# Dilated attention's transposes of p, product with V and read-out one chunk later, and modulation pieces spread anew over the steps

## The chip, the cores and the metric

The kernel runs on one core of a Trainium2 chip. The metric is the device time of one launch in microseconds (us). Five engines work from queues of their own, each strictly in its order, and wait for each other on semaphores: TensorE (PE in the profile, PEld its weight loads), VectorE (DVE), ScalarE (ACT), GpSimd (POOL) and SyncE (SP), which only issues transfers here.

## The reference, cut to what matters

Two transformer blocks over x of 256 rows and 2048 columns, in fp32. The change lies in the first, whose attention is this:

```python
mod = silu(c) @ w_ada + b_ada                       # six sections of 2048: the "modulation"
h = rms_norm(x, norm1_w) * (1 + scale1) + shift1
aq, ak, av, gq, gf, gi, gg = split(h @ w_in)        # 7 projections of 1024 columns
# 8 heads of 128; a query sees keys with a mask and a count (three dilated branches in one softmax)
p = exp(s - max(s)) * count ; o = (p @ V) / sum(p)
mix = concat(rms_norm(attn), hgrn2(gq, gf, gi, gg)) @ w_out
```

The remainder is a squared-ReLU MLP, a second block with another attention and another MLP.

## The kernel before

Weights come in chunks of 512 rows by 512 columns (1 MB). For each chunk ScalarE rounds it to w_hi (`split_hi`, L213), VectorE subtracts to get w_lo (`split_lo`, L217), and TensorE makes 24 matmuls with both (`chunk`, L227 to L229). There are four buffers, so in a step TensorE works on chunk x while the splits of chunk x+4, which take the buffer that x leaves, follow behind it.

The projection phase is a list of groups (`proj_groups`): two of HGRN2 with 16 chunks each (slots 0 to 15 and 16 to 31), then two of attention with 12 chunks each, at0 (slots 32 to 43) and at1 (slots 44 to 55). A slot is a step: one chunk on TensorE, one pair of splits. What was projected in a group is worked on in the steps of the next group: in at0's steps the second HGRN2 group runs its nine levels (`hg_stage`; level l stands on TensorE in step l, behind `grow` and copies on VectorE), in at1's steps the four heads of at0 run their softmax (`at_stage`), and the heads of at1 run it in `tail` (steps 2 to 11, slots 56 to 65), between the chunks of the output projection. After the tail VectorE squares MIX for a norm (L1133), and the late transposes and the rest of the output projection follow.

A head h of `at_stage` before the change: scores on TensorE in odd step 2h+1 (L1442, L1443); in even step 2h+2 the mask and maximum on VectorE (L1076 to L1081, signals s_max), exp on ScalarE (L626, L627), times count with the row sum on VectorE (L1085, signals p_rdy), and the three transposes of p on TensorE (L1458, wait for p_rdy); in step 2h+3 the copy of the transposes on ScalarE (L635) and the product with V (L1466 to L1468); in step 2h+4 the read-out on VectorE (L1058).

In every step an engine does its stage work first and its split after it, so ScalarE's w_hi stands behind exp, and VectorE's w_lo behind the softmax. In at0 and at1 the norm of Q or K (`head_norm`, L1008 to L1033) comes in steps 4 and 8, around that step's w_lo, with a power on GpSimd (L502) in it.

At the end of each step VectorE takes a number of modulation pieces (`ada_slot`: L902 for the first of 16, L905 for the others, 512 KB each from a ring of four that SyncE fills in order between the weight chunks). After every sixteenth piece come two collections (`ada_collect`, L890 and L892 twice). There are 96 pieces; `ada_pieces(slot)` says how many a slot has. SyncE loads x again only when all 96 are used.

Of the kernel before, what the change touches and what calls it, by code (L numbers as in the profile page):

```python
# [79 lines left out]
LEVEL_SLOTS = range(CH * 4, CH * 4 + 12), range(CH * 8, CH * 8 + 12)  # L80


def ada_pieces(slot):

    def before(x):
        return 3 * x // 2 if x <= CH * 4 else 3 * CH * 4 // 2 + 2 * (x - CH * 4) - sum(v < x for r in LEVEL_SLOTS for v in r)

    last = 2 * ADA_SLOTS
    return range(min(before(slot), last), min(before(slot + 1), last))
# [20 lines left out]
def build(nc, a, out):  # L110
    ctx = ExitStack()
    with ctx:
# [417 lines left out]
        def _(act):  # L530
# [75 lines left out]
            def at_stage(n, B0, s, stick):  # L606
                if s == 0:
                    act.wait_ge(chunk_done, 4 * (B0 + 3))
                    if isinstance(n, int) and n == 0:
# [4 lines left out]
                if s >= 2 and s % 2 == 0 and s <= 2 * GH:
# [13 lines left out]
                if s >= 3 and s % 2 == 1 and s <= 2 * GH + 1:  # L628
                    h = (s - 3) // 2
                    if stick:  # L630
                        act.wait_ge(arg_rdy, 4 * (n - AT_GROUPS) + h + 1)
                        act.activation(AMf[:, 0:384], AMf[:, 0:384], ACT.Exp).then_inc(pT_rdy, 1)
                    else:
                        act.wait_ge(pT_mm, 4 * n + h + 1)
                        act.activation(AMf[:, 0:384], bank(7, 0, 384), ACT.Copy).then_inc(pT_rdy, 1)  # L635
# [121 lines left out]
        def _(dve):  # L757
# [291 lines left out]
            def at_stage(n, s, stick, col):  # L1049
                d()  # L1050
                if s >= 4 and s % 2 == 0 and s <= 2 * GH + 2:
                    h = s // 2 - 2
                    dve.wait_ge(pv_mm, 4 * n + h + 1)
                    dst, src = MIX[:, :, col(h)], bank(7, 0, 2 * HD).rearrange("p (t d) -> p t d", t=T)
                    if stick:
                        dve.tensor_copy(dst, src).then_inc(pv_out, 1)
                    else:
                        dve.tensor_tensor(dst, src, rl[:, h % 2, :].unsqueeze(2).to_broadcast([P, T, HD]),  # L1058
                                          ALU.mult).then_inc(pv_out, 1)
                if s >= 2 and s % 2 == 0 and s <= 2 * GH:  # L1060
# [13 lines left out]
                    else:  # L1074
# [7 lines left out]
                        dve.wait_ge(p_exp, 4 * n + h + 1)  # L1082
                        for t, (c0, c1_) in enumerate(((0, 128), (128, 384))):
                            pp = E0f[:, 384 + c0:384 + c1_]
                            ins = dve.tensor_tensor_reduce(pp, pp, count[:, c0:c1_], 1.0, 0.0, ALU.mult, ALU.add,  # L1085
                                                           l_[:, t:t + 1])
                        ins.then_inc(p_rdy, 1)
                        d()
                        dve.reciprocal(rl[:, h % 2, :], l_[:, :])
                        d()  # L1090
# [247 lines left out]
        def _(pe):  # L1338
# [89 lines left out]
            def at_stage(n, s, stick):  # L1428
                if s >= 1 and s % 2 == 1 and s <= 2 * GH - 1:
# [6 lines left out]
                    if not (isinstance(n, int) and n == 0 and h == 0):  # L1436
                        pe.wait_ge(p_rdy, 4 * n + h)
# [231 lines left out]
```

## Time and profile before

| | |
|---|---|
| time, median of 3 runs | 2560.53 us (2560.37 to 2561.35) |
| the profiled execution | 2563.18 us, span 2561.1 us, mean TensorE clock 0.978 |
| TensorE busy | 2356.2 us (92%) |
| VectorE busy | 1673.7 us (65%) |
| ScalarE busy | 990.9 us (39%) |
| chain that ended last | TensorE 82%, VectorE 7% |
| mean w_lo (L217), w_hi (L213) | 2295 ns, 1915 ns |
| 1 MB of w_in from issue to landing (median) | 7.1 us |

Busy shares are of the span. A share is a mean over phases: TensorE sits still mostly in the first 700 us, in the phases that the change touches. An idle time behind a row is that of its engine just before it, with who ended it.

### The profile page before, as it was taken

The page shows a single profiled execution, that of the slowest core. Times are in us where ns is not written, and L with a number is a line of the kernel's source. Part 1 is how long each engine was busy: PE and PEld are TensorE (multiplying, and loading weights), DVE is VectorE, ACT ScalarE, POOL GpSimd, SP SyncE. Part 2 cuts the span into 40 slices and gives each one's busy share as a digit, 9 for nine tenths or more (in the row PEclk, how much of TensorE's full clock was granted, in tenths as well). Part 3 has the DMA queues.
Part 4 walks back from the last instruction along what each step waited for, and adds up shares of the span by engine and source line. Part 5 has one row for each costly group of instructions (what it writes and reads, how often), then busy time and mean ns, then how long its engine had stood idle before and what let it go on. Part 6 is the DMA issues. An engine that isn't in the chain of part 4 may idle for free.

```text
span 2561.1 us, 27768 instructions
## 1 busy us (share of the span) xinstructions
PE 2356.2 (92%) x10802; PEld 1955.8 (76%) x10802; DVE 1673.7 (65%) x1406; ACT 990.9 (39%) x745; POOL 60.1 (2%) x63
## 2 busy tenths in 40 slices
PE   0499989786899999999999999999999999999999
PEld 0488777665688888888887788877788888888887
DVE  7888797787656666665556755555765555555554
ACT  1143323233333333343433455565343334343332
POOL 0000000000000000000001200000000000000000
PEclk9999999888899999999999999999999999999999
DMA  7898575666466676755554454443555555555553
GB/s 315 329 356 298 186 262 203 204 211 214 133 215 232 228 244 232 243 190 187 191 186 148 164 179 161 158 158 115 161 198 186 193 185 194 184 193 184 193 185 110
DMA packets 230595, 519.14 MB, mean 203 GB/s; under 512 B 9402, under 2 KB 9859, under 8 KB 223875
## 3 DMA queue, kind: packets, MB, share of 16 engines
q1 hardware_dynamic: 230530, 518.27, 59.2%
q8 instruction: 42, 0.69, 0.1%
q14 instruction: 23, 0.18, 0.0%
HBM read 516.14 MB, written 2.10 MB: 202 GB/s over the span
## 4 chain that ended last, share of the span: by engine, by line
PE 82%; DVE 7%; issue 3%; ACT 2%; DMA 2%; DVEq 2%; POOL 1%; POOLq 0%; ACTq 0%; SPq 0%
PE PS L227 26%; PE PS L229 26%; PE PS L228 26%; DMA ada_raw<-in_w_ada_dram 2%; PE PS L1372 2%; ACT w_hi L213 1%; DVE ada_acc L905 1%; DVE MS L865 1%; PE PS L1405 1%; DVE GN L303 1%; POOL rstd L502 0%; DVEq L971 0%; PE PS L264 0%; DVE A_lo L311 0%; DVE w_lo L217 0%
## 5 line engine op out<-in xcount | busy, mean ns | idle before, releaser
L217 DVE TENSOR_TENSOR w_lo<-raw,w_hi 128x2048 fp32r<-128x2048 f32 x392 | 898.6, 2295 | 758.9 <-ACT w_hi L213 757.0
L213 ACT ACTIVATE w_hi<-raw 128x2048 fp32r<-128x2048 f32 x392 | 749.9, 1915 | 1172.4 <-PE PS L229 1160.8
L227 PE MATMUL PS<-w_hi,A_hi 128*128 128x512 f32 x2112 | 839.7, 398 | 21.9 <-DVE A_lo L311 15.7
L229 PE MATMUL PS<-w_hi,A_lo 128*128 128x512 f32 x2112 | 828.7, 392 | 0.0
L228 PE MATMUL PS<-w_lo,A_hi 128*128 128x512 f32 x2112 | 828.5, 392 | 0.0
L227 PEld LDWEIGHTS PS<-w_hi,A_hi 128*128 128x128 f32 x2112 | 401.7, 190 | 106.2 <-DVE A_lo L311 15.9
L229 PEld LDWEIGHTS PS<-w_hi,A_lo 128*128 128x128 f32 x2112 | 400.3, 190 | 84.9
L228 PEld LDWEIGHTS PS<-w_lo,A_hi 128*128 128x128 f32 x2112 | 401.4, 190 | 81.5 <-issue 0.5
L227 PE MATMUL PS<-w_hi,H_hi 128*128 128x512 f32 x1024 | 402.8, 393 | 0.1
L229 PE MATMUL PS<-w_hi,H_lo 128*128 128x512 f32 x1024 | 399.2, 390 | 0.0
L228 PE MATMUL PS<-w_lo,H_hi 128*128 128x512 f32 x1024 | 398.8, 389 | 0.0
L229 PEld LDWEIGHTS PS<-w_hi,H_lo 128*128 128x128 f32 x1024 | 192.5, 188 | 40.4
L227 PEld LDWEIGHTS PS<-w_hi,H_hi 128*128 128x128 f32 x1024 | 192.6, 188 | 39.8 <-issue 0.9
L228 PEld LDWEIGHTS PS<-w_lo,H_hi 128*128 128x128 f32 x1024 | 192.7, 188 | 39.5 <-issue 0.5
L905 DVE SCALAR_TENSOR_TENSOR ada_acc<-X,sc,ada_acc 128x1024 f32<-128x1024 f32 x90 | 115.3, 1281 | 3.8 <-DVE ada_acc L905 0.3
L1355 PE MATMUL PS<-ones,MS 128*128 128x1 f32 x64 | 13.9, 352 | 89.9 <-DVE MS L865 89.9
L1355 PEld LDWEIGHTS PS<-ones,MS 128*128 128x128 f32 x64 | 13.8, 332 | 90.2 <-issue 58.0
L865 DVE SCALAR_TENSOR_TENSOR MS<-ada_raw,sc,MS 128x2048 f32<-128x2048 f32 x30 | 70.5, 2351 | 3.8 <-DMA ada_raw<-in_w_ada_dram 1.6
L1218 DVE TENSOR_TENSOR X<-X,PS 128x1024 f32<-128x1024 f32 x60 | 72.8, 1214 | 0.0
L1218 DVE TENSOR_TENSOR ACC<-ACC,PS 128x1024 f32<-128x1024 f32 x60 | 72.8, 1214 | 0.0
L288 ACT ACTIVATE A_hi<-GN 128x512 fp32r<-128x512 f32 x24 | 15.1, 629 | 117.7 <-DVE GN L303 117.7
L502 POOL TENSOR_TENSOR rstd<-ssq,mhalf 128x8 f32<-128x8 f32 x19 | 33.1, 1742 | 1075.5 <-DVE ssq L328 1075.5
(250 smaller groups left out, 1175.3 us busy)
## 6 DMA issues: line engine op xcount, KB each, us to landing
raw<-in_w_ff_dram SPq DMA_DIRECT2D x128, 1024.0 KB, 5.2
raw<-in_mlp_w_in_dram SPq DMA_DIRECT2D x64, 1024.0 KB, 5.4
raw<-in_mlp_w_out_dram SPq DMA_DIRECT2D x64, 1024.0 KB, 4.9
raw<-in_w_in_dram SPq DMA_DIRECT2D x56, 1024.0 KB, 7.1
X<-in_w_ada_dram SPq DMA_DIRECT2D x96, 512.0 KB, 5.3
raw<-in_sb_w_qkv_dram SPq DMA_DIRECT2D x48, 1024.0 KB, 5.0
ada_raw<-in_w_ada_dram SPq DMA_DIRECT2D x32, 1024.0 KB, 7.2
raw<-in_w_out_dram SPq DMA_DIRECT2D x16, 1024.0 KB, 8.4
```

Source lines behind the costliest of these rows:

```text
L213: act.activation(w_hi[:, j, :, :], raw[:, j, :, :], ACT.Copy).then_inc(hi_rdy, 1)
L217: dve.tensor_tensor(w_lo[:, j, :, :], raw[:, j, :, :], w_hi[:, j, :, :].bitcast(F32), ALU.subtract).then_inc(lo_rdy, 1)
L227: pe.matmul(bank(pair + t), h, w_hi[:, j, k, :], start=first, stop=False)
L228: pe.matmul(bank(pair + t), h, w_lo[:, j, k, :], start=False, stop=False)
L229: mm = pe.matmul(bank(pair + t), l, w_hi[:, j, k, :], start=False, stop=last)
L303: ins = dve.tensor_scalar(tmp[:, pos % 2, S * k:S * k + S], bank(banks[pos % len(banks)], S * k, S * k + S), g[:, kt:kt + 1], s[:, kt:kt + ...
L502: pool.tensor_tensor(rstd[:, :], ssq[:, :], mhalf[:, :], ALU.pow).then_inc(rstd_rdy, 1)
L865: ins = dve.scalar_tensor_tensor(out=MS[:, h, :], in0=sl, scalar=sc[:, k:k + 1], in1=MS[:, h, :], op0=ALU.mult, op1=ALU.add)
L905: ins = dve.scalar_tensor_tensor(out=acc, in0=ada_ring[:, q % CH, :], scalar=sc[:, k:k + 1], in1=acc, op0=ALU.mult, op1=ALU.add)
L1218: dve.tensor_tensor(ac, ac, PS[:, b:b + 2, :], ALU.add).then_inc(acc_read, 1)
L1355: mm = pe.matmul(bank(6, KT * h + k, KT * h + k + 1), MS[:, h, k * P:k * P + P], ones[:, 0:1], start=True, stop=True)
L1372: mm = pe.transpose(bank(first_bank + i, P * q, P * q + P), src[:, t, HD * h:HD * (h + 1)], ident[:, :])
```

## The change

Part one: for the dilated attention (stick is False) `lag = s - 1` takes the place of s for count and row sum (VectorE), the transposes of p, the product with V (TensorE), the copy between them (ScalarE, now ahead of exp in a step) and the read-out (VectorE). Scores, mask, maximum and exp keep their steps, and the scores now wait for s_max in place of p_rdy. Part two: a table gives the pieces of each slot.

```diff
-LEVEL_SLOTS = range(CH * 4, CH * 4 + 12), range(CH * 8, CH * 8 + 12)
+PIECES = (1, 2) * 8 + \
+         (2, 1, 1, 1, 1, 1, 1, 1, 1, 1, 1, 0, 2, 3, 2, 3) + \
+         (2, 1, 1, 1, 0, 1, 1, 1, 0, 1, 2, 2) + \
+         (2, 2, 1, 2, 0, 2, 1, 2, 0, 2, 2, 2) + \
+         (2,) * 9 + (1,)
...
+    return range(sum(PIECES[:slot]), sum(PIECES[:slot + 1]))
...
@@ ScalarE, at_stage (the same block stood behind exp before)
+                lag = s if stick else s - 1
+                if lag >= 3 and lag % 2 == 1 and lag <= 2 * GH + 1:
+                    h = (lag - 3) // 2
...
+                        act.wait_ge(pT_mm, 4 * n + h + 1)
+                        act.activation(AMf[:, 0:384], bank(7, 0, 384), ACT.Copy).then_inc(pT_rdy, 1)
@@ VectorE, at_stage
-                if s >= 4 and s % 2 == 0 and s <= 2 * GH + 2:
-                    h = s // 2 - 2
+                lag = s if stick else s - 1
+                if lag >= 4 and lag % 2 == 0 and lag <= 2 * GH + 2:
+                    h = lag // 2 - 2
...
-                        dve.wait_ge(p_exp, 4 * n + h + 1)
-                        for t, (c0, c1_) in enumerate(((0, 128), (128, 384))):
...
+                if not stick and lag >= 2 and lag % 2 == 0 and lag <= 2 * GH:
+                    h = lag // 2 - 1
+                    dve.wait_ge(p_exp, 4 * n + h + 1)
+                    for t, (c0, c1_) in enumerate(((0, 128), (128, 384))):
@@ TensorE, at_stage
-                        pe.wait_ge(p_rdy, 4 * n + h)
+                        pe.wait_ge(p_rdy if stick else s_max, 4 * n + h)
...
-                if s >= 2 and s % 2 == 0 and s <= 2 * GH:
-                    h = s // 2 - 1
+                lag = s if stick else s - 1
+                if lag >= 2 and lag % 2 == 0 and lag <= 2 * GH:
+                    h = lag // 2 - 1
...
-                if s >= 3 and s % 2 == 1 and s <= 2 * GH + 1:
-                    h = (s - 3) // 2
+                if lag >= 3 and lag % 2 == 1 and lag <= 2 * GH + 1:
+                    h = (lag - 3) // 2
```

Before, slots 0 to 15 had 1 and 2 in turn as now, slots 16 to 27 and 32 to 43 had 1, slots 28 to 31 and 44 to 63 had 2. So the pieces of the second HGRN2 group go from 20 to 22, those of at0 from 12 to 13, of at1 from 24 to 18, of the tail from 16 to 19. The collections behind pieces 31, 47, 63, 79 and 95 move: from slot 23 to 22, from 35 to 32 (at0, step 3 to step 0), from 47 to 46 (at1, step 3 to step 2), from 55 to 57 (at1's last step to the tail), from 63 to 65.

VectorE at the turn from the last HGRN2 projection steps to at0, before: the first row is the splits of slot 31, the last the first level copy of step 1.

```order
L217 TENSOR_TENSOR w_lo<-raw,w_hi 128x2048
L905 SCALAR_TENSOR_TENSOR ada_acc<-X,sc,ada_acc 128x1024 x2
L217 TENSOR_TENSOR w_lo<-raw,w_hi 128x2048
L905 SCALAR_TENSOR_TENSOR ada_acc<-X,sc,ada_acc 128x1024
L970 TENSOR_TENSOR GN<-PS,GN 128x1024
L983 TENSOR_TENSOR AM<-PS,ident 128x1024
```

And VectorE at the same place in the changed kernel (line numbers are one higher there).

```order
L217 TENSOR_TENSOR w_lo<-raw,w_hi 128x2048
L906 SCALAR_TENSOR_TENSOR ada_acc<-X,sc,ada_acc 128x1024 x3
L217 TENSOR_TENSOR w_lo<-raw,w_hi 128x2048
L906 SCALAR_TENSOR_TENSOR ada_acc<-X,sc,ada_acc 128x1024 x2
L891 STREAM_TRANSPOSE rt<-ada_acc 128x512
L893 TENSOR_REDUCE ada_part<-rt 128x16
L891 STREAM_TRANSPOSE rt<-ada_acc 128x512
L893 TENSOR_REDUCE ada_part<-rt 128x16
L971 TENSOR_TENSOR GN<-PS,GN 128x1024
L984 TENSOR_TENSOR AM<-PS,ident 128x1024
```

Two more pieces and a pair of collections stand ahead of step 1's copy; one more piece is added in slot 29.

VectorE in at1 from step 2 on (first head of at0), before.

```order
L1076 TENSOR_TENSOR E<-PS,maskadd 128x384
L1078 TENSOR_REDUCE mx<-E 128x1
L1079 TENSOR_REDUCE mx<-E 128x1
L1081 TENSOR_SCALAR nmx<-mx 128x2
L1085 ISA E,l_<-E,count 128x128
L1085 ISA l_ 128x1
L1085 ISA E,l_<-E,count 128x256
L1085 ISA l_ 128x1
L1089 RECIPROCAL rl<-l_ 128x2
L217 TENSOR_TENSOR w_lo<-raw,w_hi 128x2048
L905 SCALAR_TENSOR_TENSOR ada_acc<-X,sc,ada_acc 128x1024 x2
```

VectorE at the same place in the changed kernel.

```order
L1083 TENSOR_SCALAR nmx<-mx 128x2
L217 TENSOR_TENSOR w_lo<-raw,w_hi 128x2048
L906 SCALAR_TENSOR_TENSOR ada_acc<-X,sc,ada_acc 128x1024
L891 STREAM_TRANSPOSE rt<-ada_acc 128x512
L893 TENSOR_REDUCE ada_part<-rt 128x16
L891 STREAM_TRANSPOSE rt<-ada_acc 128x512
L893 TENSOR_REDUCE ada_part<-rt 128x16
L1089 ISA E,l_<-E,count 128x128
L1089 ISA l_ 128x1
L1089 ISA E,l_<-E,count 128x256
L1089 ISA l_ 128x1
L1093 RECIPROCAL rl<-l_ 128x2
```

The product with count (now L1089), which the transposes wait for, has moved behind a w_lo, one piece and a pair of collections.

## Rows read from the trace of the kernel before

**Rows 1.** Timeline of TensorE, first matmul after a stall: start, us, shape, [idle <- releaser].

```profile
280.80 1.41 PE L1401 MATMUL PS<-bT,kT 128*128 128x128 f32 x5 [3.37 <-DVE AM L989]
...
346.04 2.05 PE L1405 MATMUL PS<-bT,kT 128*128 128x128 f32 x16
...
363.71 2.05 PE L1405 MATMUL PS<-bT,kT 128*128 128x128 f32 x16 [2.92 <-DVE kT L963]
...
376.94 3.78 PE L1405 MATMUL PS<-bT,kT 128*128 128x128 f32 x16 [5.71 <-DVE kT L963]
...
445.48 0.90 PE L1458 MATMUL PS<-ident,E 128*128 128x128 f32 x3 [3.95 <-DVE l_ L1085]
...
467.85 0.90 PE L1458 MATMUL PS<-ident,E 128*128 128x128 f32 x3 [6.80 <-DVE l_ L1085]
...
487.04 0.90 PE L1458 MATMUL PS<-ident,E 128*128 128x128 f32 x3 [4.46 <-DVE l_ L1085]
...
505.97 0.88 PE L1458 MATMUL PS<-ident,E 128*128 128x128 f32 x3 [3.61 <-DVE l_ L1085]
```

**Rows 2.** Timeline of TensorE inside two chunks.

```profile
413.49 0.39 PE L228 MATMUL PS<-w_lo,A_hi 128*128 128x512 f32 x1
413.72 0.39 PE L229 MATMUL PS<-w_hi,A_lo 128*128 128x512 f32 x1
...
447.03 0.63 PE L229 MATMUL PS<-w_hi,A_lo 128*128 128x512 f32 x1
447.46 0.63 PE L227 MATMUL PS<-w_hi,A_hi 128*128 128x512 f32 x1
```

**Rows 3.** Seven stretches, TensorE: length, busy, granted clock, DMA share, GB/s.

```profile
280.80:284.00 3.20, 3.20 (x12) 0.50 0.02 5
376.90:383.00 6.10, 6.06 (x22) 0.50 0.41 116
...
sum 30.60, PE 30.51; mean PE 4.36
```

**Rows 4.** Groups of instructions on VectorE from 424 to 600 us.

```profile
L905 DVE SCALAR_TENSOR_TENSOR ada_acc<-X,sc,ada_acc 128x1024 f32<-128x1024 f32 x39 | 50.0, 1282 | 2.5 <-DVE ada_acc L905 0.3
```

**Rows 5.** Timeline of VectorE, around a pair of collections.

```profile
461.28 0.71 DVE L890 STREAM_TRANSPOSE rt<-ada_acc 128x512 f32<-128x512 f32 x1
...
464.47 0.42 DVE L1058 TENSOR_TENSOR MIX<-PS,rl 128x256 f32<-128x256 f32 x1
```

**Rows 6.** Timeline of VectorE in at0, steps 2 and 4.

```profile
344.69 0.69 DVE L962 TENSOR_TENSOR bT<-bT,E 128x512 f32<-128x512 f32 x1
...
366.54 2.28 DVE L217 TENSOR_TENSOR w_lo<-raw,w_hi 128x2048 fp32r<-128x2048 f32 x1
```

**Rows 7.** One stretch: length, busy of PE, PEld, DVE, ACT, POOL, clock, DMA, GB/s.

```profile
326.00:346.00 20.00, 20.00 (x105) 16.86 (x103) 19.33 (x15) 6.66 (x4) 0.00 (x0) 1.00 0.96 362
```

**Rows 8.** Timeline of GpSimd: the powers in steps 4 and 8 of at0.

```profile
366.71 3.61 POOL L502 TENSOR_TENSOR rstd<-ssq,mhalf 128x8 f32<-128x8 f32 x1 [63.49 <-DVE ssq L328]
...
403.92 1.64 POOL L502 TENSOR_TENSOR rstd<-ssq,mhalf 128x8 f32<-128x8 f32 x1 [33.59 <-DVE ssq L328]
```

**Rows 9.** Timeline of VectorE in at1, steps 2 and 4.

```profile
442.42 0.56 DVE L1076 TENSOR_TENSOR E<-PS,maskadd 128x384 f32<-128x384 f32 x1
...
444.78 0.29 DVE L1085 CUSTOM_DVE_ANT_0 E<-E,count 128x128 f32<-128x128 f32 x1 [0.87 <-ACT E L627]
...
446.58 2.29 DVE L217 TENSOR_TENSOR w_lo<-raw,w_hi 128x2048 fp32r<-128x2048 f32 x1 [0.90 <-ACT w_hi L213]
...
472.07 1.22 DVE L1014 TENSOR_TENSOR QN<-PS,rstd 128x1024 f32<-128x1024 f32 x1
...
476.45 0.75 DVE L902 TENSOR_SCALAR ada_acc<-X,sc 128x1024 f32<-128x1024 f32 x1
```

**Rows 10.** Timeline of VectorE: start of the tail, and its end.

```profile
539.26 0.99 DVE L303 TENSOR_SCALAR GN<-PS,gmix,zero_c 128x256 f32<-128x256 f32 x2
...
598.43 1.23 DVE L1133 CUSTOM_DVE_ANT_0 QN<-MIX 128x1024 f32<-128x1024 f32 x1 [0.22 <-issue]
```

More of the change, by code:

```diff
@@ L77 @@
 WO_ORDER = [(b, k) for b in range(3) for k in (0, 1, 2)] + [(b, 3) for b in range(3)] + [(3, k) for k in range(4)]
-LEVEL_SLOTS = range(CH * 4, CH * 4 + 12), range(CH * 8, CH * 8 + 12)
+PIECES = (1, 2) * 8 + \
[3 rows of a table added]
+         (2,) * 9 + (1,)
 def ada_pieces(slot):
[L85 to L89, printed above, removed]
+    return range(sum(PIECES[:slot]), sum(PIECES[:slot + 1]))
 def ada_collected(slot):
@@ L613, in at_stage @@
                     from_pair(VN, 2, ACT.Copy, stick).then_inc(pair_read[2], 1)
+                lag = s if stick else s - 1
+                if lag >= 3 and lag % 2 == 1 and lag <= 2 * GH + 1:
+                    h = (lag - 3) // 2
+                    if stick:
+                        act.wait_ge(arg_rdy, 4 * (n - AT_GROUPS) + h + 1)
+                        act.activation(AMf[:, 0:384], AMf[:, 0:384], ACT.Exp).then_inc(pT_rdy, 1)
+                    else:
+                        act.wait_ge(pT_mm, 4 * n + h + 1)
+                        act.activation(AMf[:, 0:384], bank(7, 0, 384), ACT.Copy).then_inc(pT_rdy, 1)
                 if s >= 2 and s % 2 == 0 and s <= 2 * GH:
@@ L627, in at_stage @@
                         act.activation(E0f[:, 512:768], E0f[:, 128:384], ACT.Exp, bias=nmx[:, 1:2]).then_inc(p_exp, 1)
-                if s >= 3 and s % 2 == 1 and s <= 2 * GH + 1:
-                    h = (s - 3) // 2
[L630 to L635, printed above, removed]
             act.wait_ge(rstd_rdy, POWER_OF[0])
@@ L1081, in at_stage @@
                         dve.tensor_scalar(nmx[:, :], mx[:, :], -1.0, None, ALU.mult).then_inc(s_max, 1)
-                        dve.wait_ge(p_exp, 4 * n + h + 1)
-                        for t, (c0, c1_) in enumerate(((0, 128), (128, 384))):
[L1084 to L1090, printed above, removed]
+                if not stick and lag >= 2 and lag % 2 == 0 and lag <= 2 * GH:
+                    h = lag // 2 - 1
+                    dve.wait_ge(p_exp, 4 * n + h + 1)
+                    for t, (c0, c1_) in enumerate(((0, 128), (128, 384))):
+                        pp = E0f[:, 384 + c0:384 + c1_]
+                        ins = dve.tensor_tensor_reduce(pp, pp, count[:, c0:c1_], 1.0, 0.0, ALU.mult, ALU.add,
+                                                       l_[:, t:t + 1])
+                    ins.then_inc(p_rdy, 1)
+                    d()
+                    dve.reciprocal(rl[:, h % 2, :], l_[:, :])
+                    d()
                 if stick and s >= 3 and s % 2 == 1 and s <= 2 * GH + 1:
@@ L1459, in at_stage @@
                     mm.then_inc(pT_mm, 1)
-                if s >= 3 and s % 2 == 1 and s <= 2 * GH + 1:
-                    h = (s - 3) // 2
+                if lag >= 3 and lag % 2 == 1 and lag <= 2 * GH + 1:
+                    h = (lag - 3) // 2
                     cols = slice(HD * h, HD * (h + 1))
```

## The prediction

> **What bounds the kernel now.** I read the shares first: TensorE is busy 92% of the span and 82% of the chain that ended last, so almost all of the launch is matmul time that the change doesn't touch. What can move is TensorE's idle time. So next comes the timeline of TensorE with the idle time before each row, in the phases that the change edits. Each stall there ends with VectorE: one in the second HGRN2 group (3.4 us), two in at0 (levels 4 and 5: 2.9 and 5.7 us), four in at1 at the transposes of p (4.0, 6.8, 4.5, 3.6: 18.9 us) [rows 1]. Level 2 in at0, at 346.04, has no idle time before it [rows 1], though VectorE ran its `grow` for it only from 344.69 [rows 6]: VectorE arrives just in time there, with nothing to spare.
>
> A stall costs twice. Between two matmuls of a chunk there are 0.23 us at the full clock and 0.43 us in the step after the stall at 445.48 [rows 2]; seven stretches behind such stalls, 30.6 us in all, ran at half the granted clock (1.2 of 2.4 GHz), 4.4 us each on the mean [rows 3]. By the two intervals a stretch loses 0.47 of its length, so 2.05 us on the mean. The stall of 2.92 us was followed by no such stretch, that of 3.37 us was [rows 1, 3]. The four stalls in at1 with 18.0 us of low clock behind them thus cost 18.9 + 8.5 = 27.4 us. The Trainium skill (TensorE: Matmul & The Clock Gate, Part 1) puts the penalty at the throttled time times one half; by that a stretch would lose 2.2 us and the four in at1 9.0 us, which alters no sign below.
>
> VectorE's prices: a piece is 1.28 us busy [rows 4], 1.4 with its gap; a pair of collections takes 3.2 us [rows 5]; a w_lo 2.2 us from start to next start (table above: 2.295 busy); mask and maximum 1.5 us (442.42 to 444.78 less the 0.87 idle), count and row sums 0.7 us until TensorE's transposes at 445.48 [rows 1, 9]; norm, gain and rotation of Q or K after the w_lo 4.4 us [rows 9]. On ScalarE exp takes 0.85 us (VectorE's idle 0.87 [rows 9]) and w_hi 1.9 us (table). A chunk is 24 matmuls at 0.227, 5.45 us. Scores, transposes and product with V take about 0.5, 0.45 and 0.7 us; each is there as often after as before, so their price doesn't enter, only where they stand.
>
> **The second HGRN2 group.** The pair of collections moves from slot 23 to 22. The stall of 3.4 us before level 8 goes and one of the same 3.2 us comes before level 7, which waits for a copy that follows these collections. Sum 0. Its one more piece in slot 16 meets steps with VectorE waiting for w_hi, so it costs nothing; if that cover were gone, 1.4 us.
>
> **at0, a loss.** Three pieces (slots 29, 31, 32; one each) and a pair of collections (from step 3 to step 0) now stand before VectorE's step 1. VectorE is busy 19.3 of 20 us from 326 to 346 [rows 7], so all of it delays: 3 x 1.4 + 3.2 = 7.4 us; the piece of step 1 is then the first of its sixteen, 0.5 us shorter. `grow` of level 2 ends 6.6 to 6.9 us later, and TensorE, which was ready at 346.04, waits: +6.6, and +2.05 for the clock. Behind it level 4 no longer waits (-2.9), since the collections that made it wait are gone from step 3. Level 5 waits for all of step 4: from the end of chunk 3 VectorE needs w_hi 2.0, w_lo 2.2, piece 1.4, level work 1.4 and 1.4, squares 1.5, w_lo 2.2, a pause of 1.5, norm 4.4 and `grow` 1.2 = 19.2; TensorE needs twice a chunk and a level, 14.5. So 4.7 to 5.0 us of stall in place of 5.7, with the same low clock (-0.7). Sum: 6.6 + 2.05 - 2.9 - 0.7 = +5.05.
>
> The pause of 1.5 us is one place to weigh a rule. The power on GpSimd that began with a w_lo just under way took 3.61 us, another that began ahead of its w_lo took 1.64 [rows 6, 8]. The Trainium skill (SBUF — State Buffer, Who interferes with whom) says that VectorE and GpSimd share one pair of ports under an exclusive lock; the first row agrees with that. By the rule the pause stays, as w_hi of that step is ready before VectorE comes; by the row of 1.64 it would go, and the sum for at0 would be +3.5.
>
> **at1, a gain.** I carry the queues forward on the old clock of the trace. The one piece more of slots 42 and 43 uses up two pauses before w_lo and leaves VectorE 0.8 us late at the mask: 443.2. s_max 444.7, exp 445.55, w_hi 447.45 (VectorE has only this to wait for: 2.75 us idle in place of 0.87 + 0.90), w_lo 449.65, one piece and the collections 454.25, count and sums: p_rdy at 454.95. TensorE ends chunk 2 at 441.5 (445.48 less 3.95), chunk 3 and the scores at 447.45. It waits 7.5 us, where it waited 4.0 a step earlier: the chunk of cover is eaten by w_lo, piece and collections. Then at half clock for a while: chunk 4 ends 462.9, and chunk 5 with product and scores 469.5; VectorE: w_hi 464.9, w_lo 467.1, norm 471.5, read-out and sums 472.5, a wait of 3.0. In the same way: steps 6 and 7 without a norm, p_rdy 486.6 against 485.05, a wait of 1.55; steps 8 and 9 with the norm of K, 504.7 against 498.65, a wait of 6.05. Together 18.1 us, hardly less than 18.9, but only two of the four are long enough for the low clock for sure (4.1 us in place of 8.5); the one of 3.0 lies between 2.9 and 3.4, and I count half a stretch, 1.0 us. Sum up to step 9: 18.1 + 4.1 + 1.0 - 27.4 = -4.2. The pair of collections that stood in the last step, right before the tail's first transform, moves into the tail: -3.2. Sum -7.4.
>
> **The tail, a loss.** From its first VectorE row to the squares of MIX are 59.2 us [rows 10], nearly all VectorE's queue. It gets three pieces (4.15 us) and a pair of collections (3.2) more; all stand before the squares. The four waits for exp (3.5 us) and four for w_hi go (3.8 us); after the mask in steps 4 and 6 and in step 3 there are waits for w_hi of 2.7, 2.7 and 1.4. Sum: 7.35 - 7.3 + 6.8 = +6.85. TensorE has no chunk left to do from step 8 on, so nothing covers this. After the tail nothing is changed. SyncE's reload of x and the weights behind it wait for piece 96; it now comes about 0.6 us later relative to the squares, while the first split behind the reload stands after a norm and four transforms: nothing.
>
> **Sum.** 0 + 5.05 - 7.4 + 6.85 = +4.5 us. The profiled execution (2563.18 us, 2.65 above the median) would take 2567.7; the median 2565.0. A measurement of this kernel tells about 0.2%, 5.1 us, from no change; +4.5 is just inside.
>
> **Bounds.** A low-clock stretch is between 3.2 and 6.1 us long, so each of the six in question may cost 1.5 to 2.9: about +-1.5 in all. If the 3.0 us wait keeps the full clock, -1.0. Small restart costs of each stall that I left out: -1. At the turn to at0 three-piece slots make SyncE, which serves the ring and the weights in one order, issue weight loads later: 1 MB takes 7.1 us to land (table), and the DMA engines are 0.96 busy from 326 to 346 us already [rows 7]. If the loads for slots 34 to 36 land late, VectorE's full queue gets up to 3 us longer.
>
> **Rivals.** (1) At0 costs little: if VectorE had slack before level 2 that I don't see, at most 5.05 goes and the sum is -0.5: 2560.0. Against it: no idle time between `grow` at 344.69 and the level at 346.04 [rows 1, 6]. (2) The other side, faster: the extra chunk covers the K norm in step 9. If VectorE comes to its product there 6 us earlier than I count, the wait of 6.05 and its low clock (2.05) go, the sum is -3.6; it decides for faster from the point on where the waits of steps 3 or 5 also go, together -8 to -14: 2550. For it: the wait is a difference of two long queues, and one chunk more is what the transposes get. Against: before, the wait with the norm of Q in the same step was the longest [rows 1], and w_hi behind exp keeps VectorE idle longer than before. (3) Slower: the loads of slots 34 to 36 come late as above and each new stall draws the longest low clock: +3, +3.5: +11, 2571.5. (4) The lag does nothing because all depends on the pieces: then at1 gives only -3.2, and the sum is +8.7, 2569.
>
> **Chances.** The forecast (+2 to +7) 0.5, half a step under the 5.1 us border, so 0.27 within and 0.23 slower; (1) 0.16 within; (2) 0.13, faster; (3) and (4) 0.21, slower. That is 0.13 faster, 0.43 within, 0.44 slower. The range leaves out the far part of (2) and (3): 2556 to 2571.
>
> **What would show it.** TensorE: a new stall of 6 to 7 us before level 2 in at0 (near 353 us), none before level 4; in at1 waits for L1089's signal in steps 3, 5, 7, 9 of about 7.5, 3, 1.5 and 6 us; the tail's first transform on VectorE about 2 us earlier than 539.3, and the squares 66 us after it, near 603. VectorE idle about 2.7 us before w_lo in steps 2 and 6 of at1. Wrong would be: no stall at level 2, a wait in step 9 under 3 us, or a tail under 63 us.

## The result, and the profile after

The changed kernel took 2572.09 us (median of 6 runs, 2570.87 to 2574.16), the kernel before 2561.38 beside it: ratio 1.004, 95% interval 1.003 to 1.005. It is 10.7 us slower; the forecast was +4.5. The profiled execution took 2572.91 us, its span 2570.9 us. The instructions are as many as before. TensorE is busy 2.1 us longer and stands still 7.7 us longer (the span less its busy time, 212.6 us after 204.9):

```profile
span 2570.9 us, 27768 instructions
...
PE 2358.3 (92%) x10802; PEld 1958.8 (76%) x10802; DVE 1674.2 (65%) x1406; ACT 991.6 (39%) x745; POOL 62.0 (2%) x63
```

The timeline of TensorE in the kernel after, the first matmul behind each wait (the counterpart of [rows 1]; columns as there):

```profile
273.08 3.44 PE L1409 MATMUL PS<-bT,kT 128*128 128x128 f32 x16 [3.66 <-DVE AM L990]
...
354.19 3.78 PE L1409 MATMUL PS<-bT,kT 128*128 128x128 f32 x16 [8.60 <-DVE kT L964]
...
383.43 3.78 PE L1409 MATMUL PS<-bT,kT 128*128 128x128 f32 x16 [5.03 <-DVE kT L964]
...
461.50 0.90 PE L1463 MATMUL PS<-ident,E 128*128 128x128 f32 x3 [7.47 <-DVE l_ L1089]
...
479.10 0.90 PE L1463 MATMUL PS<-ident,E 128*128 128x128 f32 x3 [3.34 <-DVE l_ L1089]
...
494.56 0.56 PE L1463 MATMUL PS<-ident,E 128*128 128x128 f32 x3
...
513.96 0.90 PE L1463 MATMUL PS<-ident,E 128*128 128x128 f32 x3 [7.19 <-DVE l_ L1089]
```

Two things are to be seen. Level 2 of at0, which waited for nothing before, waits 8.60 us; level 4 has no wait any more, level 5 has 5.03. In at1 the four waits at the transposes are now three, 18.0 us together against 18.8 [rows 1], though each transpose has a chunk of matmuls more ahead of it.

VectorE's timeline gives the start and the end of the tail (counterpart of [rows 10]): 67.21 us where there were 59.17. The row between them is the tail's first w_lo.

```profile
539.49 0.99 DVE L303 TENSOR_SCALAR GN<-PS,gmix,zero_c 128x256 f32<-128x256 f32 x2
...
554.40 2.29 DVE L217 TENSOR_TENSOR w_lo<-raw,w_hi 128x2048 fp32r<-128x2048 f32 x1 [2.94 <-ACT w_hi L213]
...
606.70 1.23 DVE L1137 CUSTOM_DVE_ANT_0 QN<-MIX 128x1024 f32<-128x1024 f32 x1 [0.22 <-issue]
```

Part by part, from the same events in both traces (a part is how much later its last event comes, less what the parts before it added):

| part | forecast | measured | from which events |
|---|---|---|---|
| second HGRN2 group | 0 | -0.45 | w_hi at 289.08, after 288.63 |
| at0 | +5.05 | +6.9 | at1's first scores 435.25, after 441.66 |
| at1 | -7.4 | -6.2 | tail's first transform 539.26, after 539.49 |
| tail | +6.85 | +8.0 | 59.17 and 67.21 us |
| behind the tail | 0 | +1.6 | first transpose of ACC 678.54, after 688.37 |
| sum | +4.5 | +9.8 | |

The three parts with a forecast other than 0 have its sign: the two that cost came out dearer, and the one that pays paid less. Behind the tail, where nothing was forecast, 1.6 us came. The forecast 2565.0 missed by 7.1 us, 1.1 beyond its range. Of these, 0.85 us are the kernel before, whose median beside this one is 2561.38 and not 2560.53; as a difference the forecast is 6.2 us off. The two traces differ by 9.8 us and the medians by 10.7, because the profiled execution of the kernel before took 1.8 us more than its median and that of the kernel after 0.8.

Two readings show the excess. First, ScalarE's timeline ahead of the new wait in at0, and VectorE's beside it:

```profile
327.53 1.92 ACT L213 ACTIVATE w_hi<-raw 128x2048 fp32r<-128x2048 f32 x1 [5.11 <-DMA raw<-in_w_in_dram]
337.10 1.92 ACT L213 ACTIVATE w_hi<-raw 128x2048 fp32r<-128x2048 f32 x1 [6.74 <-DMA raw<-in_w_in_dram]
...
339.05 2.29 DVE L217 TENSOR_TENSOR w_lo<-raw,w_hi 128x2048 fp32r<-128x2048 f32 x1 [1.73 <-ACT w_hi L213]
```

w_hi waits for a transfer of weights (five do between 320 and 348 us; in the kernel before none does from 260 to 700 us), and VectorE, in a stretch in which it was to be full, waits 1.73 us for w_hi. Second, TensorE's granted clock. Stretches of the kernel before (columns as in [rows 7]) at the tail's first chunk and behind the tail:

```profile
543.50:550.50 7.00, 6.99 (x24) 5.66 (x25) 5.39 (x15) 1.46 (x4) 0.00 (x0) 0.75 0.00 0
604.50:614.50 10.00, 8.43 (x36) 6.79 (x37) 7.45 (x13) 6.51 (x8) 0.00 (x0) 0.80 0.76 295
```

and the same two places in the kernel after:

```profile
543.70:550.70 7.00, 6.95 (x18) 5.47 (x19) 6.27 (x11) 1.49 (x4) 0.00 (x0) 0.56 0.21 65
612.70:622.70 10.00, 8.45 (x29) 6.69 (x30) 7.40 (x13) 6.52 (x8) 0.00 (x0) 0.56 0.83 321
```

In 7 and 10 us it did 24 and 36 matmuls before, 18 and 29 after: at mean clocks of 0.56 instead of 0.75 and 0.80. The waits ahead of these places were 8.95 and 12.71 us before, 7.48 and 13.87 after, nearly the same. What differs is how long the half clock lasts behind them.

### The profile page after: what moved, and what is told of

Its sections match the earlier page's. It is cut to its first block, busy times and chain, and to the rows that moved or that the text cites. A ratio compares the mean times of both kernels' runs of the same rounds, so it can differ in the third digit from the quotient of the medians.

```text
span 2570.9 us, 27768 instructions
## 1 busy us (share of the span) xinstructions
PE 2358.3 (92%) x10802; PEld 1958.8 (76%) x10802; DVE 1674.2 (65%) x1406; ACT 991.6 (39%) x745; POOL 62.0 (2%) x63
## 4 chain that ended last, share of the span: by engine, by line
PE 80%; DVE 8%; issue 4%; ACT 2%; DMA 2%; DVEq 2%; POOL 1%; POOLq 0%; ACTq 0%; SPq 0%
PE PS L227 25%; PE PS L229 25%; PE PS L228 25%; DVE ada_acc L906 2%; ACT w_hi L213 2%; PE PS L1376 2%; DVE MS L866 1%; DMA ada_raw<-in_w_ada_dram 1%; PE PS L1409 1%; DVE GN L303 1%; DVE w_lo L217 1%; POOL rstd L502 0%; DVEq L890 0%; PE PS L264 0%; DVE A_lo L311 0%
```

## The experiments

Each was timed beside the kernel before, whose median stood between 2561.1 and 2561.7 us; the kernel after is 2572.1. Each kernel has one trace; where a run's times scatter widely, its trace need not stand for its median.

### One half of the change at a time

e1 has the lag alone, with the pieces of before:

```diff
-PIECES = (1, 2) * 8 + \
...
+LEVEL_SLOTS = range(CH * 4, CH * 4 + 12), range(CH * 8, CH * 8 + 12)
...
```

> The kernel before with the lag of one chunk alone: transposes, product with V and read-out come a chunk later, the modulation pieces stay where they were. Theory (the lag pays only together with its spread, since the queue of VectorE between two masks doesn't get shorter): carrying the queues forward with the old spread gives waits of TensorE at the transposes in at1 of 4.9, 8.4, 1.4 and 8.9 us, 23.6 in all against 18.9 before, one low-clock stretch fewer, and a tail about 1 us longer; at0 and the second HGRN2 group as before. Sum about +3.5 on the kernel before: 2565. Rival (the chunk of cover is worth something by itself): the four waits shrink by more than 5 us in all with their low-clock stretches, 2556 or less. The kernel after stood at 2572.1.

It took 2565.56 us (ratio 1.0017, 1.0008 to 1.0026). The timeline of TensorE in e1, in at1:

```profile
452.53 0.90 PE L1463 MATMUL PS<-ident,E 128*128 128x128 f32 x3 [4.68 <-DVE l_ L1089]
...
475.91 0.90 PE L1463 MATMUL PS<-ident,E 128*128 128x128 f32 x3 [7.78 <-DVE l_ L1089]
...
491.38 0.55 PE L1463 MATMUL PS<-ident,E 128*128 128x128 f32 x3 [1.24 <-DVE l_ L1089]
...
512.44 0.90 PE L1463 MATMUL PS<-ident,E 128*128 128x128 f32 x3 [8.89 <-DVE l_ L1089]
```

22.6 us against 18.8, where 23.6 was forecast: the theory's queues hold within a microsecond. The lag alone costs 4.0 us.

e2 has the table of pieces alone, in the order of before:

```diff
-LEVEL_SLOTS = range(CH * 4, CH * 4 + 12), range(CH * 8, CH * 8 + 12)
+PIECES = (1, 2) * 8 + \
+         (2, 1, 1, 1, 1, 1, 1, 1, 1, 1, 1, 0, 2, 3, 2, 3) + \
...
```

> The kernel before with the new table of modulation pieces alone; transposes, product and read-out stay where they were. Theory (the spread makes the loss, in at0 and the tail, and the lag gives little back): at0 +6.5 to +8.5 at level 2 as in the kernel after, the tail about 3 pieces and a pair of collections longer (+6 to +7), at1's waits of TensorE shorter only by the collections taken out (-3): 2569 to 2571. Rival (the lag makes the loss): 2563 or less.

2569.53 us (1.0021 to 1.0048): the spread alone costs 8.0 us. Its wait at level 2 was 8.70 us (8.60 after), and its tail 66.1 us (67.2 after). The halves together would be +12.0, and both are +10.7: each loses by itself, and they give each other back little.

### What stands ahead of level 2

```diff
-         (2, 1, 1, 1, 1, 1, 1, 1, 1, 1, 1, 0, 2, 3, 2, 3) + \
+         (2, 1, 1, 1, 1, 1, 1, 1, 1, 2, 1, 1, 2, 2, 2, 2) + \
```

> The kernel after with no slot of three pieces: two pieces of the last steps before at0's first chunks go to earlier steps of the second HGRN2 group. The slots from 16 on are 2 1 1 1 1 1 1 1 1 2 1 1 2 2 2 2 instead of 2 1 1 1 1 1 1 1 1 1 1 0 2 3 2 3. Theory (two pieces of VectorE's full queue and the late weight loads behind the threes make a part of at0's new stall at level 2): VectorE no longer idles 1.7 us for w_hi before level 2, and its queue has two pieces (2.8 us) less there; the stall of 8.6 us becomes 4 to 5, and the time falls by 4.5 to 2567.6. Rival (it comes back as a stall in the second HGRN2 group or at level 5, where TensorE waits for VectorE anyway): 2571 to 2572.

2566.86 us: 5.2 less than after, 4.5 forecast. The wait at level 2 fell from 8.60 to 4.19 us, and nothing came back in the HGRN2 group (3.65 us in place of 3.66).

e4 leaves the table and moves the piece loads behind the next weight load on SyncE:

```diff
                     load(B, j, w_in[:, j, :, c0:c0 + NC_])
-                    if B:
-                        for q in ada_pieces(CH * (B - 1) + j):
+                    if B and CH * (B - 1) + j:
+                        for q in ada_pieces(CH * (B - 1) + j - 1):
                             ada_load(q)
...
```

> The kernel after with one thing changed on SyncE: the loads of a slot's modulation pieces are issued one weight load later, so that the weight load of the next step stands ahead of them in the ring. Theory (weight loads late behind nine piece loads of three slots hold ScalarE's w_hi at 337.10 by 6.74 us and leave VectorE idle 1.73 us before level 2): ScalarE's w_hi there no longer waits for a transfer, the stall before level 2 is 6.9 instead of 8.6 us, time 2570.4. Rival (the transfers are bound by the DMA engines, and order alone moves no weight earlier; or the loads of the pieces are then late themselves): no change, 2572, or a new wait of VectorE for a piece.

No w_hi waited for a transfer any more, and the wait at level 2 was 6.96 us, 0.06 from the forecast of 6.9:

```profile
353.74 3.77 PE L1412 MATMUL PS<-bT,kT 128*128 128x128 f32 x16 [6.96 <-DVE kT L967]
```

So the late weights make 1.64 us of that wait. The median, 2571.34 us, is only 0.75 below after, too little to be told from nothing. e17 below makes the same edit where more is late.

### The clock

e5 keeps TensorE busy in its wait behind the tail; `warm(k)` is k transposes of the identity into bank 6:

```diff
...
+            pe.wait_ge(s_max, 4 * AT_GROUPS)
+            warm(20)
             pe.wait_ge(pv_out, 4 * AT_GROUPS)
+            warm(65)
+            pe.wait_ge(rstd_rdy, POWER_OF[1])
+            warm(10)
             turn(1, MIX, steps=LATE1, first=len(EARLY1), banks=NARROW)
```

> The kernel after, and TensorE does idle work (95 transposes of the identity matrix into bank 6, which nobody reads) in the 13.9 us in which it waits for the squares of MIX at the end of the tail, in three groups held back by signals that it waits for anyway. Nothing else waits for them. Theory (1.6 us behind the tail are low clock: in the kernel after the first 3.7 us of the chunk behind this wait ran at half clock, in the kernel before none of it): the chunk runs at the full clock from its start, from the first transpose of MIX to those of ACC 74.0 us in place of 75.6, time 1.6 to 2.2 below the kernel after: 2570.2. Rival (the chunk is held by VectorE's splits and the queue behind it, not by TensorE's clock): less than 0.5 us, 2571.7 or more.

2573.7 us, nothing gained. The idle work did lift the clock inside the wait, but it fell again right at the chunk. Stretches of e5:

```profile
602.00:612.00 10.00, 8.20 (x74) 7.76 (x73) 7.07 (x12) 0.31 (x1) 1.64 (x1) 1.00 0.70 267
...
612.90:617.90 5.00, 2.50 (x18) 1.70 (x16) 4.01 (x8) 3.10 (x6) 0.00 (x0) 1.00 1.05 408
618.60:622.00 3.40, 3.40 (x9) 2.63 (x8) 2.19 (x5) 2.89 (x3) 0.00 (x0) 0.50 0.71 275
```

Between the idle work and the chunk TensorE has only the 16 transposes of MIX, with pauses: busy 2.5 of 5 us. Behind these the clock was low for 3.4 us, in the chunk, where the kernel after has 3.5 us of low clock. So the run tells nothing about the price of the low clock there; it shows that this idle work, which ended 5 us ahead of the chunk, did not shorten the low clock in it.

e6 does the same inside at1's waits, where the next work follows at once:

```diff
...
             def at_stage(n, s, stick):
+                if isinstance(n, int) and n == 0 and not stick and s in (3, 5, 9):
+                    pe.wait_ge(s_max, 4 * n + s // 2)
+                    warm({3: 60, 5: 24, 9: 60}[s])
```

> The kernel after, and TensorE does idle work (transposes of the identity into bank 6, 60, 24 and 60 of them) ahead of the scores in steps 3, 5 and 9 of at1, within its waits of 7.5, 3.3 and 7.2 us, so that its clock doesn't fall behind them. In the kernel after 14.2 us behind these three waits ran at half clock, by the two intervals of [rows 2] 6.7 us. Theory (the time lost to the clock is in part time that TensorE would wait for VectorE in the next step: the queue of VectorE sets the steps, and only what is lost behind the last wait, or what VectorE waits for in turn, is paid): waits become longer by part of it, 3.5 to 4.5 us are gained, 2568. Rival (as the prediction reckoned, a low-clock stretch adds in full to its wait): 6.7 us, 2565.4. Other rival (VectorE alone sets at1): under 1 us, 2571.5.

2568.84 us (8 runs, 2564.51 to 2573.01). Stretches of the kernel after behind its three waits:

```profile
461.50:464.60 3.10, 3.10 (x9) 2.62 (x10) 2.99 (x3) 0.49 (x1) 0.00 (x0) 0.50 0.73 274
479.10:485.00 5.90, 5.90 (x16) 4.75 (x17) 5.52 (x6) 0.49 (x1) 0.00 (x0) 0.50 0.16 28
514.00:519.20 5.20, 5.20 (x18) 4.62 (x19) 4.93 (x4) 1.58 (x3) 0.00 (x0) 0.50 0.07 9
```

and the same places in e6:

```profile
462.30:465.40 3.10, 3.09 (x15) 2.61 (x16) 2.98 (x3) 0.49 (x1) 0.00 (x0) 1.00 0.79 297
480.00:485.90 5.90, 5.90 (x21) 4.75 (x22) 5.55 (x6) 0.49 (x1) 0.00 (x0) 0.71 0.19 33
513.60:518.80 5.20, 5.20 (x29) 4.50 (x30) 4.93 (x4) 1.58 (x3) 0.00 (x0) 1.00 0.10 17
```

65 matmuls in place of 43 in the same 14.2 us. A half clock of 3.4 us stayed behind the second wait (the mean of 0.71), so 10.8 us of low clock went, worth 5.1 us at 0.47. Gained were 3.3 us by the medians and 4.3 by the trace, from the transposes in step 3 to the squares (145.2 to 140.9 us). The first theory's 3.5 to 4.5 fits better than the full price, but the runs of e6 scatter over 8.5 us, and the trace is of the slowest of them: the 76.9 us from the first transpose of MIX to those of ACC are the most of all traces here, and its whole span, 2571.0 us, is that of the kernel after. So this is a hint and not a proof that a part of each low-clock stretch is time that TensorE would have waited anyway.

### Who eats the chunk of cover

The change moved the count and the read-out on VectorE along with TensorE's transposes: the count now stands behind w_lo, the pieces and the collections of its step. e9 undoes that part alone:

```diff
             def at_stage(n, s, stick, col):
-                lag = s if stick else s - 1
-                if lag >= 4 and lag % 2 == 0 and lag <= 2 * GH + 2:
-                    h = lag // 2 - 2
+                if s >= 4 and s % 2 == 0 and s <= 2 * GH + 2:
+                    h = s // 2 - 2
...
-                if not stick and lag >= 2 and lag % 2 == 0 and lag <= 2 * GH:
-                    h = lag // 2 - 1
+                if not stick and s >= 2 and s % 2 == 0 and s <= 2 * GH:
+                    h = s // 2 - 1
```

> The kernel after with one part of the lag undone: on VectorE count, row sums and read-out stay in the steps of before (right behind the mask, ahead of w_lo and pieces); on TensorE and ScalarE transposes, the copy of p and the product come a chunk later, the pieces are spread as after. Theory (the chunk of cover is eaten because the same edit puts VectorE's count behind w_lo, the pieces and a read-out that itself comes late): TensorE's waits in at1 shrink from 18 us to 6 or 7 (half of that moves to the scores, which wait for the mask), and the time falls to 2560 to 2562. Rival (VectorE's queue is full in at1, so that its order is all the same): waits of 15 us or more, 2569 or more. Other rival (VectorE now waits for the product in the step in which it reads it out, up to 10 us in the tail): 2572 or more.

2559.4 us: 12.7 less than after, and level with before (ratio 0.9994, 0.9985 to 1.0003). TensorE's timeline in at1 of e9, the four transposes and, of the scores, the two that wait:

```profile
453.06 0.49 PE L1462 MATMUL PS<-ident,E 128*128 128x128 f32 x3
...
466.24 0.49 PE L1445 MATMUL PS<-kT,qT 128*128 128x128 f32 x2 [1.07 <-DVE nmx L1082]
...
467.76 0.55 PE L1462 MATMUL PS<-ident,E 128*128 128x128 f32 x3 [0.59 <-DVE l_ L1088]
...
483.38 0.49 PE L1445 MATMUL PS<-kT,qT 128*128 128x128 f32 x2 [3.45 <-DVE nmx L1082]
...
484.89 0.90 PE L1462 MATMUL PS<-ident,E 128*128 128x128 f32 x3 [0.50 <-DVE l_ L1088]
...
498.11 0.49 PE L1462 MATMUL PS<-ident,E 128*128 128x128 f32 x3
```

5.6 us of waits in place of 18.0, where 6 to 7 were forecast. From the first scores of at1 to the tail's first transform e9 takes 82.6 us, the kernel after 97.8. In the tail VectorE waits once 3.23 us for the product, and the tail is 1.4 us longer than after. A chunk of cover is worth a chunk once the signal that it covers isn't put off by the same edit. e10 is the same with the pieces of before:

```diff
-PIECES = (1, 2) * 8 + \
...
+LEVEL_SLOTS = range(CH * 4, CH * 4 + 12), range(CH * 8, CH * 8 + 12)
```

> The kernel before with transposes, copy of p and product a chunk later on TensorE and ScalarE alone; VectorE's order and the pieces as before. Theory as for e9: the four waits of TensorE at the transposes in at1 (18.9 us before) come down to under 2 us, 3 to 6 us come back as waits for the mask, and waits behind the last K norm grow (one of 5 to 8 us before the tail's first chunk): 5 to 6 us below the kernel before, 2555.5, and 10 below the lag with VectorE in it (e1, 2565.6). Rival (any lag costs): 2562 or more.

2558.28 us, 7.3 less than e1, 2.9 under before, where 5 to 6 were forecast. Its waits at the transposes in at1 are 2.1 us in all, but its tail takes 63.9 us, with a wait for the count of 9.54 us.

e13 and e15 take the lag out of the tail, in the kernel after and in e10 (the first pair of lines wherever it stands):

```diff
-                lag = s if stick else s - 1
+                lag = s if stick or n else s - 1
-                        pe.wait_ge(p_rdy if stick else s_max, 4 * n + h)
+                        pe.wait_ge(p_rdy if stick or n else s_max, 4 * n + h)
```

> The kernel after with the lag in at1 only: in the tail (the second attention group, after the last projection step) transposes, copy, product, count and read-out stand in the steps of before. Theory (with no chunk of projection behind it, the lag in the tail costs VectorE about 1 us, and it is also what makes the chunk behind the tail run its first 3.7 us at half clock): tail 1 us shorter, from the first transpose of MIX to those of ACC 74.0 us in place of 75.6, time 2569.4 (2.7 less than after). Rival (the clock behind the tail falls as it does by chance of its place in time): 2571.

2571.21 us, tail 67.0 us: in the kernel after the lag costs the tail next to nothing, and the rival was right. The half clock behind the tail stayed though this lag was gone, so it doesn't need it.

> The order of e10 in at1, the order of before in the tail, the pieces as before. e10 had a wait of 9.5 us for count in its tail (the kernel before 4.9) and 75.7 us from the first transpose of MIX to those of ACC (before 74.0). Theory (both come of the lag in the tail, where no chunk covers anything): 4 us less tail and 1.6 us less behind it, 2552.7 (5.6 under e10's 2558.3, 8.5 under before). Rival (the tail's lag costs nothing, VectorE's queue there is full anyway): 2557 to 2558.

2552.71 us (ratio 0.997, 0.9959 to 0.9981), where 2552.7 was forecast; its seven times lie between 2550.2 and 2557.2, so that the match to the hundredth is luck. In e10 the tail's count stands early on VectorE while TensorE takes it up late; there the lag did cost (tail 59.1 us in place of 63.9).

### What the spread is worth

e7 is the kernel before with another table, e8 the kernel after with one, e12 a second table for the order of before, e11 one for the order of e10, e14 one for that of e15. Each table was found for its own order, by carrying the queues forward. The edit in all is of this kind (here e11, in the kernel of e9; the other tables stand in the expectations):

```diff
-         (2, 1, 1, 1, 1, 1, 1, 1, 1, 1, 1, 0, 2, 3, 2, 3) + \
-         (2, 1, 1, 1, 0, 1, 1, 1, 0, 1, 2, 2) + \
-         (2, 2, 1, 2, 0, 2, 1, 2, 0, 2, 2, 2) + \
-         (2,) * 9 + (1,)
+         (3, 0, 2, 2, 1, 2, 2, 3, 4, 4, 0, 1, 3, 1, 1, 1) + \
+         (2, 0, 1, 0, 0, 2, 2, 2, 0, 1, 1, 3) + \
+         (1, 0, 3, 1, 0, 0, 0, 3, 0, 0, 3, 0) + \
+         (4, 3, 0, 2, 2, 1, 1, 2, 2, 0)
```

> The kernel before with another table of modulation pieces; transposes, product and read-out stay in their steps of before. From slot 16 on: 2 2 1 2 1 2 1 1 3 4 2 0 3 3 0 1, then 0 1 1 0 0 4 2 2 0 2 1 2, then 1 0 4 2 1 0 3 0 0 4 0 0, then 3 1 1 2 2 1 2 1 1 0. It was found by carrying the queues of VectorE, ScalarE, TensorE and the DMA ring forward with the durations of the trace of before. Theory (VectorE's pieces in the tail and behind a norm stand in TensorE's way, and the last steps of the second HGRN2 group and steps without a norm have room): 15 to 30 us below the kernel before, 2532 to 2547. Rival (steps of three and four pieces make the weight loads late, as seen in the kernel after at 337.10, and new stalls take what the tail gives): 2555 to 2565.

> The kernel after (everything of the product one chunk later) with a table of pieces found in the same way for this order. From slot 16 on: 3 1 3 1 2 1 1 2 4 2 1 3 3 1 1 2, then 0 0 2 0 0 3 1 1 1 1 2 3, then 0 0 0 1 2 4 0 0 0 4 4 0, then 2 1 2 0 4 1 1 1 0 0. Theory (the lag itself is worth nothing or costs a few us, whatever the spread): 3 to 5 us above e7. Rival (the lag pays with the right spread): level with e7 or below it.

> The order of e10 with a table of pieces found for it by carrying the queues forward, from slot 16 on: 3 0 2 2 1 2 2 3 4 4 0 1 3 1 1 1, then 2 0 1 0 0 2 2 2 0 1 1 3, then 1 0 3 1 0 0 0 3 0 0 3 0, then 4 3 0 2 2 1 1 2 2 0. Theory (once the spread is right, the order of the product matters by 3 us and no more; both are bound by the same full queues of VectorE and TensorE): 2538 to 2544, next to e7 (2543.1). Rival (three and four pieces in slots 23 to 25 make weights late again): 2548 or more.

> As e7 (the kernel before with another table of pieces), with a table from a longer search, from slot 16 on: 2 1 2 2 2 2 1 2 4 2 3 2 0 4 2 0, then 0 1 2 0 0 2 1 1 1 1 2 2, then 0 0 4 0 1 0 4 0 3 4 0 0, then 3 1 2 1 2 1 2 0 0 0. Theory (the gain of e7 is that of the spread, not of its particular numbers): within 3 us of e7, 2540 to 2546. Rival (e7's numbers fit by luck): 2550 or more.

> The order of e15 (lag on TensorE and ScalarE in at1 only) with a table of pieces found for it, from slot 16 on: 3 0 3 2 3 1 1 2 4 4 0 3 1 0 0 3, then 2 1 1 0 0 2 3 1 2 1 4 3, then 0 1 0 2 0 0 2 0 0 1 0 0, then 4 1 2 2 0 3 0 2 0 2. Theory: by the queues it is 1 us above e11, and it gives back the 1.6 us behind the tail: 2534 to 2537, level with e11 (2536.1). Rival (its slots of four pieces, 24, 25 and 42, make weights late): 2540 or more.

e7 took 2543.12 us (ratio 0.9931), e12 2544.23, e8 2546.15, e11 2536.09 (0.9905, 0.989 to 0.992), e14 2540.33. In every order the spread is worth 12 to 26 us (12.4 from e15 to e14, 25.9 from the kernel after to e8), the order 3 to 13: the change's own lag costs 3.0 us with a table made for it (e8 over e7) and 4.0 with the old one (e1 over before), and the lag without VectorE's part gains with either. Two forecasts missed: e11 came out under its 2538 to 2544, 7.0 us below e7 where the order was to matter by 3 at most, and e14 above its 2534 to 2537, as its rival had it. The gain lies in at1: from its first scores to the tail's first transform the kernel before takes 104.0 us, e7 82.3 and e11 72.0. Before had 24 pieces there, e7 has 15 and e11 11, and the second HGRN2 group took most of them (28 and 30 in place of 20). No run moved these pieces alone. e11 is the chip's answer to what the change set out to do: TensorE's transposes in at1 (446.95, 459.56, 472.17, 484.94) wait for nothing but 0.65 us in the last:

```profile
472.17 0.49 PE L1462 MATMUL PS<-ident,E 128*128 128x128 f32 x3
...
484.94 0.55 PE L1462 MATMUL PS<-ident,E 128*128 128x128 f32 x3 [0.65 <-DVE l_ L1088]
```

e16 and e17 are e11 and e14 with e4's order on SyncE:

```diff
...
-                        for q in ada_pieces(CH * (B - 1) + j):
+                        for q in ada_pieces(CH * (B - 1) + j - 1):
...
```

> e11 with SyncE's order of e4: the loads of a slot's pieces one weight load later. In e11 one w_hi of ScalarE waited 8.6 us for its weights (303.31) and VectorE had nothing waiting behind it at this place that the end depends on. Theory (late weights cost only where VectorE's queue is full behind them, as before level 2 in the kernel after): within 2 us of e11, 2534 to 2538. Rival (they cost wherever they are late): 2533 or less.

> e14 with the same change. e14 came out 4 us above its forecast of 2536; four w_hi of ScalarE waited for weights (304.54 8.7 us, 314.24 3.1, 345.44 6.4, 439.70 4.5). Theory (this is what it lost): VectorE no longer waits for those w_hi, 2536 to 2538.5. Rival (it lost its time to the wait of 7.8 us before the tail's first chunk and to low clock): 2539.5 or more.

e16 took 2535.08 us, e17 2537.23: 1.0 and 3.1 less. In e14 four w_hi waited for weights, the first of them with VectorE behind it:

```profile
306.49 2.29 DVE L217 TENSOR_TENSOR w_lo<-raw,w_hi 128x2048 fp32r<-128x2048 f32 x1 [2.07 <-ACT w_hi L213]
```

In e17 no w_hi waits for a transfer, and that w_lo begins at 304.56 with no idle time. So late weights do cost, where VectorE's queue is full behind them. e16 (ratio 0.9898, 0.9882 to 0.9915) and e11 can't be told apart and have the lowest medians of all, with e17 one to two us above them.

## Why the prediction was wrong

The queues were right in the main: the new wait at level 2, the waits in at1 and the longer tail that they gave are all in the trace. What failed is the price of TensorE's half clock, most plainly the 0 behind the tail, and next to it the late weights, which stood among the rivals and not in the sum. Of the 5.3 us between +4.5 and the +9.8 of the traces, late weights are about 1.7 and the half clock about 4, with 0.45 the other way.

- **Second HGRN2 group, 0.** Right: a wait of 3.66 us before level 7 in place of 3.37 before level 8, -0.45 in all.
- **At0, +5.05.** The step was right (a new wait at level 2, none at level 4, 5.03 at level 5), its size 1.8 too small. The wait was to be 6.6 us and was 8.60: 1.73 of it is the late weights, which the prediction had as rival (3) and left out of its sum. e4 shows it: with the weights first, 6.96. The pause of about 1.5 us behind w_lo stayed (1.53), as the forecast had taken it by [rows 8]: the power in step 4, which began at 373.87 with a w_lo under way since 373.70, again took 3.61 us, that of step 8 1.64 (rows below). The Trainium skill (SBUF — State Buffer, Who interferes with whom) calls the port pair of VectorE and GpSimd an exclusive lock; the trace agrees again.

```profile
373.87 3.61 POOL L502 TENSOR_TENSOR rstd<-ssq,mhalf 128x8 f32<-128x8 f32 x1 [71.09 <-DVE ssq L328]
...
410.31 1.64 POOL L502 TENSOR_TENSOR rstd<-ssq,mhalf 128x8 f32<-128x8 f32 x1 [32.82 <-DVE ssq L328]
...
377.51 1.23 DVE L1015 TENSOR_TENSOR QN<-PS,rstd 128x1024 f32<-128x1024 f32 x1 [1.53 <-POOL rstd L502]
```

- **At1, -7.4.** The waits were forecast as 7.5, 3.0, 1.55 and 6.05, 18.1 us; measured 7.47, 3.34, 0 and 7.19, 18.0 us. The reason given for it (the chunk of cover is eaten by w_lo, piece and collections) is shown by e9. That the sums of the waits agree to 0.1 us is in part luck: the third was to be 1.55 and is 0, the fourth 6.05 and is 7.19. The mis-sized term is the low clock: 5.1 us by the forecast, 14.2 x 0.47 = 6.7 by the rows. The wait of 3.34 us, counted with half a stretch, drew the longest one, 5.9 us.
- **Tail, +6.85.** VectorE's three pieces and the collections are there: e2, with no lag, has a tail of 66.1 us. The other 1.2 us are the first chunk of the tail: half clock for 6.2 us in place of 3.5. It shows as VectorE's wait for w_hi in step 3, 2.94 us where 1.4 was forecast. Runs with the same tail bear it out: e6, with 4.8 us of half clock there, waits 2.30 us and has a tail of 66.6; e2 and e13, alike from the tail on, have 3.5 and 6.2 us of half clock and wait 1.40 and 2.63 us. This term isn't in the sum at all. (The waits for w_hi that go are three in the trace of before, 1.97, 0.91 and 0.90, and not four; their sum of 3.8 us is right.)
- **Behind the tail, 0.** This is the step that failed outright. "Nothing is changed" was true of the work, and the time grew by 1.6 us: the chunk starts 5.4 us behind the first transpose of MIX in both kernels, but counted from that transpose the half clock lasts 3.9 us before, and is over when the chunk starts, and 8.9 us after, which is 3.5 us of the chunk; 3.5 x 0.47 = 1.6. Of the 19 kernels with a profile here, 5 take 74.0 us from that transpose to those of ACC (before, e2, e7, e12, e15), the other 14 75.2 to 76.9. In the five the half clock ends within 4.0 us of the transpose; in 13 of the others it ends 8.3 to 11.5 us behind it, and in e5 3.4 us of it lie in the chunk.
- **The sum.** +4.5 forecast, +9.8 measured: +1.8 mostly by late weights, +1.2 and +1.2 and +1.6 mostly by low clock, -0.45. Rival (3), +11 and 2571.5 us, named both mechanisms and is nearest to what came, 2572.1, though with 3 us for the late weights, which cost about 1.7. Its chance was set too low, because its terms were counted as bounds about a middle, while late weights can only cost.

What sets the half clock's length behind the tail stays open. It doesn't need the lag: e13 and e15 have the order of before in the tail. Stretches of e13 and of e15, from the first transpose of MIX:

```profile
613.10:623.10 10.00, 8.44 (x29) 6.62 (x30) 7.40 (x13) 6.51 (x8) 0.00 (x0) 0.54 0.82 317
```

```profile
591.50:601.50 10.00, 8.37 (x36) 6.81 (x37) 7.43 (x13) 6.51 (x8) 0.00 (x0) 0.81 0.77 298
```

The same work, and clocks of 0.54 and 0.81. e2 and e13 are a closer pair, with the same table and the same order from the tail on: there the half clock ends 3.8 and 9.1 us behind the transpose, and the stretch up to ACC takes 74.0 and 75.8 us. But the lag isn't excluded as a part of the cause either: of the eleven kernels with the lag in the tail none has the 74.0 us, of the eight without it five have. That the place in time at which TensorE resumes decides is a guess that fits the pair; no run moved that place alone. The Trainium skill (TensorE: Matmul & The Clock Gate, Part 1) says that the number of matmuls at the low clock, counted from a kernel's start, varies between runs of the same kernel. No run here shows that, since each kernel has one trace.

## What to carry to other kernels

When a consumer is moved later to give it cover, leave its producer where it was: the gain is the distance between the two, and moving both along with a full queue in between gave next to nothing (18.0 us of waits after 18.8, against 5.6 in e9). Try first where small jobs stand in a full engine's queue: that was worth up to 26 us here, who waits for whom one chunk sooner or later 3 to 13. And put the low-clock stretch behind a wait into the sum in all the places where TensorE resumes, the unchanged ones too, with the longest length seen in the trace as its upper bound.

## What was not expected of the hardware

The half clock behind a wait is not a fixed price. Behind waits of 3.34, 7.19 and 7.47 us it lasted 5.9, 5.2 and 3.1 us: the shortest wait had the longest stretch. Idle work in a wait (TensorE busy 8.2 us of 10) brought the full clock back, but it didn't last into the chunk: 5 us in which TensorE was busy for 2.5 were followed by 3.4 us at half clock just when the chunk had begun.
